# The adaLN conditioning product of a two-layer decoder trunk: from VectorE multiply-adds to TensorE column strips

## The chip, the cores and the metric

The kernel runs on one core of a Trainium2 chip. The metric is the device time in microseconds of one execution, from the first to the last instruction of the program. The core has five engines with queues of their own: TensorE (PE in the profile; PEld is its weight load), VectorE (DVE), ScalarE (ACT), GpSimd (POOL) and SyncE (SP), which here issues most DMAs.

## The reference, in short

Two residual layers over 512 positions of 1024 channels. Each layer takes six vectors of 1024 numbers (shift, scale and gate of its two sub-layers) from a conditioning vector `c`:

```
cond = silu(c)                                   # (1, 1024)
for layer in range(2):
    mod = cond @ w_ada[layer] + b_ada[layer]     # w_ada[layer]: 1024 x 6144
    sh1, sc1, g1, sh2, sc2, g2 = split(mod, 6)
    u = rms_norm(h, norm_mix[layer]) * (1 + sc1) + sh1
    mix = attention and convolution of u @ w_in, times w_out   # layer 0
        or the multi-scale pooling mixer                       # layer 1
    h = h + g1 * mix
    u = rms_norm(h, norm_ffn[layer]) * (1 + sc2) + sh2
    h = h + g2 * grouped_moe(u)                  # 16 experts, top 2
out = rms_norm(h, norm_final)
```

Everything is fp32. The product with `w_ada` is a vector times a matrix: 50.3 MB are read, and each number is used once.

## The kernel before

Every engine has one instruction stream, and its order is written out by hand; semaphores tie the streams together. The order around the change is this.

*First stage.* SyncE loads `x` (four tiles of 512 KB) and the first six chunks of `w_ada`. A chunk is 384 columns of all 1024 rows, 1.5 MB, loaded as two halves of four rows per partition (`load_ada`); there are two chunk buffers, `adaw`. The rows 8p to 8p + 7 of the matrix lie on partition p, so the 128 partitions read places 192 KB apart, in both kernels. ScalarE and VectorE normalise the four tiles of `x` (`norm`). Then VectorE multiplies and adds (`ada_mul`, lines 812 to 838): for each k, 128 x 384 weights times the partition's `cond[:, k]`, into two accumulators, which it adds at the end. In the first six chunks two of the eight k go to TensorE instead (line 1203, one output row). TensorE then sums the accumulator over the partitions with a column of ones (`ada_total`, line 1206, one output row of `ps5`), ScalarE copies the row and stores it to `mod_dram` (`ada_out`). When six chunks, 2304 columns, are stored, GpSimd reads shift and scale back by columns (`load_cols`), VectorE makes the scale, ScalarE and VectorE spread the normalised and transposed tiles (`spread_all`), and the projections begin (`project`, line 1314).

*Projections and attention.* Six projections of 128 output channels come first, then nine rounds (units) of attention: scores, the transposed probabilities of the unit before, a projection, the attention product, a projection. Units 6 to 8 have no projections; halves of the output product (`mix_half`, line 1373) stand in their place. Between these pieces are 33 places, six after the projections and three per unit, and the lists `BY_PROJ` and `BY_UNIT` say how many of the remaining 26 chunks VectorE takes in at each:

```
BY_PROJ = [1, 1, 1, 1, 2, 2]
BY_UNIT = [1, 1, 0, 1, 1, 1, 1, 1, 0, 1, 1, 1, 1, 1, 0, 1, 1, 1, 1, 1, 0, 1, 0, 0, 0, 0, 0]
```

TensorE's totals and ScalarE's copies follow up to two chunks later at the same places (`place_totals`). SyncE's queue holds, in order, the chunks and between them the five pieces of `w_in` (9.4 MB) and the two of `w_out` (3 MB and 1 MB); it waits where a buffer isn't free yet, and everything behind it waits too. A place's VectorE work on attention is `soften` (lines 912 to 930: the added distance penalty, the maxima and small operations) and `divide`; its share of the projections is `empty`.

*After.* From about 306 us on come the routing, the 16 experts of layer 0 from 341 us, and layer 1. None of this is touched, but the pooling matrices and the scale of layer 1 are loaded into the space of `adaw` once the last chunk has been used.

Of the kernel before, what the change touches and what calls it, by code (L numbers as in the profile page):

```python
# [26 lines left out]
ALU = mybir.AluOpType  # L27
# [14 lines left out]
MACS = [sum(K_VEC[:n]) for n in range(LAYERS * NCH + 1)]  # L42
# [25 lines left out]
def trunk(nc, x, c, w_ada, b_ada, norm_mix, norm_ffn, w_in, w_out, sinks, conv_w, w_pool, pool_scale,  # L68
          w_router, b_router, w_gate, w_up, w_down, norm_final, consts, pool_mats, out, mod_dram, xhat_dram, h_dram):
    ctx = ExitStack()  # L70
    with ctx:
# [32 lines left out]

        adaw = sb("adaw", [P, 2, KD, AC])
        wpool = adaw[:, 0].rearrange("p k n -> p (k n)")[:, 0:KD * 256].rearrange("p (a n) -> p a n", a=KD)
        pmat = adaw[:, 1].rearrange("p k n -> p (k n)")[:, D:D + 4 * M_END].rearrange("p (g n) -> p g n", g=4)
        acc = sb("acc", [P, 4, AC])
        brow = sb("brow", [P, 2, AC])
        mrow = sb("mrow", [1, 2, AC])  # L110
# [48 lines left out]
        psc = adaw[:, 1].rearrange("p k n -> p (k n)")[:, 0:D]  # L159
        gmix = [gbc[:, :], acc[:, :, :].rearrange("p a n -> p (a n)")[:, 0:D]]  # L160
# [8 lines left out]
        craw = sb("craw", [P, KD])  # L169
        modc = sb("modc", [P, 4, 2, KD])  # L170
# [37 lines left out]
        ada_in = [sem(f"ada_in{b}{half}") for b in range(2) for half in "ab"]  # L208
# [6 lines left out]
        mac_step = sem("mac_step")  # L215
        ada_mac = sem("ada_mac")
        ada_sum = sem("ada_sum")
        row_copied = sem("row_copied")
# [74 lines left out]
        assert N_FIRST + sum(PLACES) == LAYERS * NCH  # L293

        def place_chunks(i):
            at = N_FIRST + sum(PLACES[:i])
            return range(at, at + PLACES[i])

        def place_totals(i):
            def summed(i):  # L300

                if i < 0:
                    return N_FIRST
                if i == len(PLACES) - 1:
                    return LAYERS * NCH
                return max(N_FIRST, place_chunks(i - 2).stop if i >= 2 else 0, place_chunks(i).stop - LAG)
            return range(summed(i - 1), summed(i))
# [4 lines left out]
        WO_AT = [18, 28]  # L312

        def mod_waits(eng, n):

            for q in (n, n - 1):
                eng.wait_ge(mod_stored[q % 2], 16 * (q // 2 + 1))
# [43 lines left out]
        def _(sp):  # L361
            def load_ada(n):

                b, l, q = n % 2, n // NCH, n % NCH
                if n == 0:
                    sp.wait_ge(brow_clear, 1)
                for half in range(2):
                    ks = slice(half * KD // 2, (half + 1) * KD // 2)
                    if n >= 2:

                        sp.wait_ge(mac_step, MACS[n - 1] if half else MACS[n - 2] + KD // 2)
                        if half and K_VEC[n - 2] < KD:
                            sp.wait_ge(ada_sum, n - 1)
                    sp.dma_start(adaw[:, b, ks], w_ada[l, :, q * AC:(q + 1) * AC].rearrange("(p k) n -> p k n", k=KD)
                                 [:, ks]).then_inc(ada_in[2 * b + half], 16)
                    if half == 0:
                        sp.dma_start(brow[0:1, b, :], b_ada[l:l + 1, q * AC:(q + 1) * AC]).then_inc(ada_in[2 * b], 16)
# [22 lines left out]

            for n in range(N_FIRST):
                load_ada(n)

            wsrc = w_in[0].rearrange("(p k) n -> p k n", k=KD)
            sp.dma_start(win_qkv[:, :, 0:2 * P], wsrc[:, :, 0:2 * P]).then_inc(win_in["q"], 16)
# [4 lines left out]
            for n in range(N_FIRST, LAYERS * NCH):  # L410
# [16 lines left out]
            sp.wait_ge(ada_mac, LAYERS * NCH)  # L427
# [40 lines left out]
        def _(pool):  # L468
            def load_cols(s, last_chunk):

                l, half = s // 2, s % 2
                mod_waits(pool, l * NCH + last_chunk)
# [7 lines left out]
            def load_gate(l, half):  # L480
                off = (3 * half + 2) * D
                mod_waits(pool, l * NCH + ((off + D - 1) // AC))
# [3 lines left out]
            load_cols(0, N_FIRST - 1)  # L486
# [8 lines left out]
            for l in range(LAYERS):  # L495
                if l == 0:
                    load_cols(1, (5 * D - 1) // AC)
# [6 lines left out]
                if l == 0:  # L504

                    load_cols(2, N_FIRST - 1)
                    load_cols(3, (5 * D - 1) // AC)
                    mod_waits(pool, LAYERS * NCH - 1)
                    load_gate(1, 0)
# [55 lines left out]
        def _(act):  # L565
# [26 lines left out]
            def ada_out(n):  # L592

                b, l, q = n % 2, n // NCH, n % NCH
                act.wait_ge(ada_sum, n + 1)
                if n >= 2:
                    act.wait_ge(mod_stored[b], 16 * (n // 2))
# [1023 lines left out]
```

## Time and profile before

| | us |
|---|---|
| median of 3 runs | 823.69 |
| lowest and highest run | 820.74, 826.4 |
| span of the profiled execution, first to last instruction | 823.5 |
| TensorE busy in it | 699.7 |
| VectorE busy in it | 384.1 |
| ScalarE, GpSimd busy | 181.9, 115.1 |
| first projection starts at | 59.4 |
| routing starts near, experts of layer 0 near | 306, 341 |

The profiled execution is known by its span, and that span lies among the three runs. Busy time of an engine is the union of its instructions. The granted clock is the share of TensorE's full clock, 2.4 GHz, in a stretch: 1.00 is that level and 0.50 the lower one of 1.2 GHz. An fp32 matmul of 512 columns leaves two records, one per pass. The last number of a window row is what the DMA engines moved, in GB/s. "A <- B" behind a waiting instruction names who released it.

### The profile page before, as it was taken

What the parts mean: (1) busy time and instruction counts of PE and PEld (TensorE: products, weight loads), DVE (VectorE), ACT (ScalarE), POOL (GpSimd) and SP (SyncE); (2) the same over time, 40 slices, a digit from 0 to 9 for tenths busy, and PEclk for the clock granted to TensorE, in tenths of its full rate; (3) what the DMA queues carried; (4) which work ended last, traced back from release to release, by engine and by line L of the source; (5) the groups of instructions that cost most, each with busy time, mean ns of one, the idle gap of its engine ahead of it and who ended that gap; (6) DMA issues with size and microseconds to landing.
All of it is one profiled execution on the core that took longest, in us unless ns stands there. A gap on an engine that the chain in (4) does not pass through costs nothing. (4 is left out here: it accounts for less than half of the span.)

```text
span 823.5 us, 7489 instructions
## 1 busy us (share of the span) xinstructions
PE 699.7 (85%) x2448; PEld 359.3 (44%) x2448; DVE 384.1 (47%) x796; ACT 181.9 (22%) x468; POOL 115.1 (14%) x90
## 2 busy tenths in 40 slices
PE   1569969999999994799999999479559999999960
PEld 0224434444444454455455554168534555445530
DVE  1756479998996245522232222225563323233222
ACT  3021113222221222221122211155221221122212
POOL 0000000010111003212212221100220122221110
PEclk9989969999999995799999999889559999999995
DMA  8759999865866129648888992297531889888526
GB/s 279 234 197 371 374 356 319 294 192 167 270 210 254 75 103 354 240 172 322 307 317 318 335 338 69 34 371 300 217 117 62 319 331 334 318 315 311 172 33 218
DMA packets 74977, 204.27 MB, mean 248 GB/s; under 512 B 13185, under 2 KB 48193, under 8 KB 62657
## 3 DMA queue, kind: packets, MB, share of 16 engines
q1 hardware_dynamic: 59872, 183.60, 59.7%
q0 software_dynamic: 10160, 19.46, 9.6%
q10 hardware_dynamic: 4912, 0.82, 0.6%
q8 instruction: 16, 0.26, 0.1%
q14 instruction: 17, 0.13, 0.0%
HBM read 193.04 MB, written 27.31 MB: 268 GB/s over the span
## 5 line engine op out<-in xcount | busy, mean ns | idle before, releaser
L1461 PE MATMUL ps<-ring,work 128*128 128x512 f32 x384 | 169.1, 593 | 0.0
L1314 PE MATMUL psY<-xu,ring 128*128 128x512 f32 x272 | 122.7, 606 | 1.5 <-ACT xu L627 1.5
L1461 PEld LDWEIGHTS ps<-ring,work 128*128 128x128 f32 x384 | 73.0, 191 | 90.0 <-issue 89.9
L834 DVE SCALAR_TENSOR_TENSOR acc<-adaw,cond,acc 128x384 f32<-128x384 f32 x180 | 98.6, 611 | 4.5 <-DMA adaw<-in_w_ada_dram 4.4
L1090 DVE TENSOR_TENSOR work<-work,ps 128x256 f32<-128x256 f32 x32 | 13.5, 421 | 177.9 <-ACT work L731 177.8
L522 POOL DMA_INDIRECT h_dram<-work x32 | 50.6, 1581 | 304.0 <-DVE work L1109 275.7
L1484 PE MATMUL psY<-ring,work 128*128 128x512 f32 x192 | 86.6, 594 | 1.2 <-ACT work L741 1.2
L1314 PEld LDWEIGHTS psY<-xu,ring 128*128 128x128 f32 x272 | 51.2, 193 | 69.1 <-issue 66.2
L1109 DVE SCALAR_TENSOR_TENSOR work<-psY,work,gbc 128x512 f32<-128x512 f32 x64 | 45.1, 746 | 74.0 <-PE psY L1484 74.0
L731 ACT ACTIVATE work<-ps 128x256 f32<-128x256 f32 x32 | 12.3, 385 | 270.6 <-PE ps L1461 270.6
L725 ACT ACTIVATE work<-psA,modc,scl 128x128 f32<-128x128 f32 x120 | 45.2, 457 | 51.5 <-PE psA L1451 51.5
L1461 PE MATMUL ps<-xu,work 128*128 128x512 f32 x128 | 56.2, 592 | 0.0
L1484 PEld LDWEIGHTS psY<-ring,work 128*128 128x128 f32 x192 | 34.6, 190 | 36.0 <-issue 34.4
L1083 DVE TENSOR_SCALAR work<-psA,scl,modc 128x128 f32<-128x128 f32 x120 | 41.0, 404 | 15.7 <-PE psA L1451 14.6
L1206 PE MATMUL ps<-acc,cst 128*1 128x384 f32 x64 | 29.1, 539 | 18.5 <-DVE acc L838 15.5
L1373 PE MATMUL psY<-ring,work 128*128 128x512 f32 x96 | 42.8, 597 | 1.8 <-DVE h L872 1.8
L533 POOL DMA_INDIRECT work<-xhat_dram,work x32 | 35.5, 1110 | 46.6 <-DVE work L1070 37.5
L1461 PEld LDWEIGHTS ps<-xu,work 128*128 128x128 f32 x128 | 24.3, 190 | 30.6 <-issue 30.6
L1451 PE MATMUL psA<-cst,work 128*128 128x128 f32 x240 | 33.4, 284 | 3.1 <-DMA work<-xhat_dram,work 3.1
L493 POOL TENSOR_TENSOR work<-work,sm 128x1024 f32<-128x1024 f32 (+1 forms) x8 | 14.3, 1790 | 155.2 <-DVE sm L936 155.2
L598 ACT ACTIVATE mrow<-ps 1x384 f32<-1x384 f32 x32 | 15.2, 476 | 92.5 <-PE ps L1206 90.1
L828 DVE SCALAR_TENSOR_TENSOR acc<-adaw,cond,brow 128x384 f32<-128x384 f32 x32 | 21.4, 668 | 25.7 <-DMA brow<-in_b_ada_dram 25.5
(154 smaller groups left out, 696.1 us busy)
## 6 DMA issues: line engine op xcount, KB each, us to landing
adaw<-in_w_ada_dram SPq DMA_DIRECT2D x64, 768.0 KB, 6.1
ring<-in_w_gate_dram SPq DMA_DIRECT2D x24, 1024.0 KB, 4.9
ring<-in_w_up_dram SPq DMA_DIRECT2D x24, 1024.0 KB, 7.0
ring<-in_w_down_dram SPq DMA_DIRECT2D x24, 1024.0 KB, 11.4
ring<-in_w_in_dram SPq DMA_DIRECT2D x4, 2048.0 KB, 13.6
xu<-in_w_gate_dram SPq DMA_DIRECT2D x8, 1024.0 KB, 4.8
xu<-in_w_up_dram SPq DMA_DIRECT2D x8, 1024.0 KB, 6.9
xu<-in_w_down_dram SPq DMA_DIRECT2D x8, 1024.0 KB, 11.3
```

Source lines behind the costliest of these rows:

```text
L522: pool.indirect_dma_start(out=h_dram[l], out_offset=bass.IndirectOffsetOnAxis(tok_i[:, e:e + 1], 0), in_=yrow[:, e % 2, :], in_offset=None ...
L533: pool.indirect_dma_start(out=xg[:, e % 4, :], out_offset=None, in_=xhat_dram[l], in_offset=bass.IndirectOffsetOnAxis(tok_i[:, e:e + 1], 0 ...
L725: ins = act.activation(xgT[:, j % 2, k, :], turned_ps(e)[:, k * P:(k + 1) * P], ACT.Identity, scale=scl[:, 2 * l + 1, k:k + 1], bias=modc[ ...
L834: ins = dve.scalar_tensor_tensor(part, adaw[:, b, k, :], cond[:, k:k + 1], part, ALU.mult, ALU.add)
L1083: ins = dve.tensor_scalar(xgT[:, j % 2, k, :], turned_ps(e)[:, k * P:(k + 1) * P], scl[:, 2 * l + 1, k:k + 1], modc[:, 2 * l + 1, 0, k:k + 1],
L1109: ins = dve.scalar_tensor_tensor(yrow[:, j % 2, a * 512:(a + 1) * 512], psY[:, a * 512:(a + 1) * 512], gslot[:, bass.ds(e, 1)], gbc[:, a * ...
L1206: pe.matmul(ps5[0:1, 0:AC], ones[:, 0:1], acc[:, n % 3, :], start=(K_VEC[n] == KD), stop=True).then_inc(ada_sum, 1)
L1314: ins = pe.matmul(bank, wt, uT[:, k, :], start=(k == 0), stop=(k == KD - 1))
L1373: ins = pe.matmul(ps[:, a * 512:(a + 1) * 512], lhs, wo[:, q, a * 512:(a + 1) * 512], start=(q == 0), stop=(q == 7))
L1451: ins = pe.transpose(turned_ps(e)[:, k * P:(k + 1) * P], xg[:, j % 4, :].rearrange("p (a k) -> p k a", k=KD)[:, k, :], ident)
L1461: ins = pe.matmul(gu_ps[j % 2][:, :].rearrange("p (a f) -> p a f", a=2), xgT[:, j % 2, k, :], w_gu(j % 4)[:, :, k, :], start=(k == 0), sto ...
L1484: ins = pe.matmul(psY[:, a * 512:(a + 1) * 512], hT[:, q, :], w_dn(j)[:, q, a * 512:(a + 1) * 512], start=(q == 0), stop=(q == 1))
```

## The change

The conditioning product goes to TensorE altogether. `cond` is widened once to 32 equal columns (`condw`). The matrix is taken in slices of 1 MB: one of the eight rows of each partition, 2048 columns wide, one run of 8 KB per partition. Eight slices make a bank of 2048 columns, there are three banks per layer, 48 slices in all, and three buffers of a slice. For each slice TensorE runs four matmuls, each of 512 columns and with 32 equal stationary columns, into the four strips of 32 partitions of `ps5`; over the eight slices they accumulate, so that partitions 0, 32, 64 and 96 hold the row. VectorE adds the bias from PSUM (`row_sum`), and ScalarE stores the four pieces (`row_out`). The order of SyncE's loads, the places and the transposes of the first stage move with it, and SyncE no longer waits for the first shift and scale ahead of the second piece of `w_in`. Shortened where "..." stands:

```diff
-AC = 384
-NCH = MODW // AC
-N_FIRST = 6
-K_VEC = [KD - 2 if n < N_FIRST else KD for n in range(LAYERS * NCH)]
+AC = 512
+AG = 4
+BANK = AG * AC
+NB = MODW // BANK
+NSL = LAYERS * NB * KD
+ABUF = 3
...
+        condw = sb("condw", [P, KD, 32])
...
-        LAG = 2
-        BY_PROJ = [1, 1, 1, 1, 2, 2]
-        BY_UNIT = [1, 1, 0, 1, 1, 1, 1, 1, 0, 1, 1, 1, 1, 1, 0, 1, 1, 1, 1, 1, 0, 1, 0, 0, 0, 0, 0]
+        BY_PROJ = [1, 1, 2, 2, 2, 2]
+        BY_UNIT = [2, 2, 1] * 6 + [0] * 9
...
-        WO_AT = [18, 28]
+        WO_AT = [21, 46]
...
             def load_ada(n):
...
+                b, bank, k = n % ABUF, n // KD, n % KD
+                l, q = bank // NB, bank % NB
+                if n >= ABUF:
+                    sp.wait_ge(ada_mm, n - ABUF + 1)
+                sp.dma_start(adaw[:, b, :], w_ada[l, :, q * BANK:(q + 1) * BANK].rearrange("(p k) n -> p k n", k=KD)
+                             [:, k]).then_inc(ada_in[b], 16)
+                if k == 3:
+                    if bank == 0:
+                        sp.wait_ge(brow_clear, 1)
+                    else:
+                        sp.wait_ge(row_ready, bank)
+                    sp.dma_start(brow[0:P:32, :],
+                                 b_ada[l, q * BANK:(q + 1) * BANK].rearrange("(a n) -> a n", a=AG)
+                                 ).then_inc(brow_in, 16)
...
-            for n in range(N_FIRST):
+            wsrc = w_in[0].rearrange("(p k) n -> p k n", k=KD)
+            for n in range(KD):
+                if n == KD - 2:
+                    sp.dma_start(win_qkv[:, :, 0:2 * P], wsrc[:, :, 0:2 * P]).then_inc(win_in["q"], 16)
                 load_ada(n)
...
-            sp.wait_ge(modc_in[0], 32)
             sp.dma_start(win_qkv[:, :, 2 * P:B0], wsrc[:, :, 2 * P:B0]).then_inc(win_in["qkv"], 16)
...
-                for name, place, dst, at0 in (("c", 3, win_c, C0), ("x", 4, win_x, X0), ("b", 5, win_b, B0)):
-                    if n == N_FIRST + place:
+                for name, place, dst, at0 in (("c", 4, win_c, C0), ("x", 6, win_x, X0), ("b", 8, win_b, B0)):
+                    if n == KD + place:
...
+            def row_out(n):
+
+                l, q = n // NB, n % NB
+                act.wait_ge(row_ready, n + 1)
+                act.dma_start(mod_dram[l, q * BANK:(q + 1) * BANK].rearrange("(a n) -> a n", a=AG),
+                              mrow[0:P:32, n % 2, :]
+                              ).then_inc(mod_stored[n % 2], 16)
...
+            def row_sum(n):
...
+                dve.wait_ge(ada_mm, (n + 1) * KD)
+                dve.wait_ge(brow_in, 16 * (n + 1))
+                if n >= 2:
+                    dve.wait_ge(mod_stored[b], 16 * (n // 2))
+                dve.tensor_tensor(mrow[:, b, :], ps5[:, :], brow[:, :], ALU.add).then_inc(row_ready, 1)
...
+            def ada_slice(n):
+
+                bank, k = n // KD, n % KD
+                if n == 0:
+                    pe.wait_ge(condw_ready, 1)
+                if k == 0 and bank:
+                    pe.wait_ge(row_ready, bank)
+                pe.wait_ge(ada_in[n % ABUF], 16 * (n // ABUF + 1))
+                for a in range(AG):
+                    ins = pe.matmul(ps5[32 * a:32 * a + 32, :], condw[:, k, :],
+                                    adaw[:, n % ABUF, a * AC:(a + 1) * AC], start=(k == 0), stop=(k == KD - 1))
+                ins.then_inc(ada_mm, 1)
...
-            for n in range(N_FIRST):
-                if n == 2:
+            for n in range(KD):
+                if n == 4:
                     transposes_all(range(KD - 1))
-                ada_total(n)
-            pe.wait_ge(row_copied, N_FIRST)
+                ada_slice(n)
+            pe.wait_ge(row_ready, 1)
             keep_clock(4, ps5[:, :])
             transposes_all(range(KD - 1, KD))
```

At the places TensorE calls `ada_slice` for each slice of `place_slices`, and VectorE and ScalarE call `row_sum` and `row_out` where the eighth slice of a bank stands.

## Rows read from the trace of the kernel before

**Rows 1.** Windows: span, busy PE, PEld, DVE, ACT, POOL; clock, DMA share, GB/s.
```profile
0.00:59.43 59.43, 26.76 (x77) 8.09 (x77) 29.90 (x60) 13.98 (x26) 1.53 (x6) 0.94 0.72 230
59.43:114.00 54.57, 47.41 (x156) 22.68 (x156) 29.76 (x58) 5.99 (x11) 0.53 (x1) 0.96 1.05 374
114.00:127.80 13.80, 11.78 (x28) 4.85 (x28) 13.59 (x31) 3.88 (x12) 0.00 (x0) 0.68 0.92 301
127.80:231.20 103.40, 102.17 (x339) 45.22 (x338) 94.64 (x190) 24.15 (x72) 10.23 (x6) 1.00 0.73 243
231.20:306.00 74.80, 72.95 (x255) 35.28 (x254) 41.49 (x82) 21.37 (x54) 5.13 (x4) 1.00 0.47 170
```
**Rows 2.** TensorE's waits (total, times, longest), 56 to 125 us, then 118 to 300.
```profile
PE ps L1206 <- DVE acc L838: 7.4, 2, 5.4
...
PE ps L1206 <- DVE acc L838: 2.0, 1, 2.0
...
PE ps L1206 <- ACT mrow L598: 1.2, 1, 1.2
```
**Rows 3.** Timeline to the first projections: start, duration, engine, line.
```profile
21.14 0.75 DVE L843 TENSOR_SCALAR xu<-h,rstd 128x1024 f32<-128x1024 f32 x1
...
50.30 1.21 PE L1206 MATMUL ps<-acc,cst 128*1 128x384 f32 x2
52.08 3.70 PE L1193 MATMUL ps<-cst 128*128 128x512 f32 x8 [0.57 <-ACT mrow L598]
53.46 1.33 POOL L478 DMA_DIRECT2D modc<-mod_dram  x2 [52.93 <-DMA mod_dram<-mrow]
59.43 20.84 PE L1314 MATMUL psY<-xu,ring 128*128 128x512 f32 x48 [1.53 <-ACT xu L627]
```
**Rows 4.** Timeline of TensorE, the end of the first projections.
```profile
112.64 1.44 PE L1206 MATMUL ps<-acc,cst 128*1 128x384 f32 x2 [5.42 <-DVE acc L838]
...
117.27 1.44 PE L1206 MATMUL ps<-acc,cst 128*1 128x384 f32 x2 [2.02 <-DVE acc L838]
118.64 9.17 PE L1314 MATMUL psY<-xu,ring 128*128 128x512 f32 x16
```
**Rows 5.** Timeline of TensorE, the end of unit 3 and the start of unit 4.
```profile
182.19 1.58 PE L1354 MATMUL ps<-work 128*64 128x128 f32 x16
183.70 7.13 PE L1314 MATMUL psY<-xu,ring 128*128 128x512 f32 x16
190.77 0.81 PE L1206 MATMUL ps<-acc,cst 128*1 128x384 f32 x2
191.50 1.14 PE L1329 MATMUL psA<-work 64*128 64x256 f32 x8
...
192.57 0.66 PE L1341 MATMUL ps<-cst,work 128*128 128x128 f32 x4
```
**Rows 6.** Groups by line, 59 to 272 or 310 us: busy, mean ns, idle before.
```profile
L1206 PE MATMUL ps<-acc,cst 128*1 128x384 f32 x52 | 22.2, 510 | 10.4 <-DVE acc L838 7.4 <-ACT mrow L598 3.0
...
L834 DVE SCALAR_TENSOR_TENSOR acc<-adaw,cond,acc 128x384 f32<-128x384 f32 x156 | 85.0, 610 | 0.1
...
L910 DVE TENSOR_TENSOR work<-work,psY 128x512 f32<-128x512 f32 x4 | 2.7, 670 | 0.6 <-PE psY L1314 0.6
L921 DVE SCALAR_TENSOR_TENSOR work<-cst,psA 128x128 f32<-128x128 f32 x8 | 1.8, 281 | 0.0
...
L926 DVE TENSOR_REDUCE sm<-work 128x4 f32<-128x512 f32 x2 | 1.4, 686 | 0.1
```
**Rows 7.** Windows as in rows 1: x, chunks alone, expert weights.
```profile
2.00:10.00 8.00, 0.00 (x0) 0.00 (x0) 0.51 (x3) 1.33 (x2) 0.00 (x0) 1.00 0.99 365
10.00:18.00 8.00, 2.72 (x4) 0.37 (x4) 0.92 (x2) 3.97 (x8) 0.00 (x0) 1.00 1.07 330
...
320.00:324.00 4.00, 0.22 (x8) 0.23 (x9) 3.60 (x13) 0.00 (x0) 0.00 (x0) 0.50 1.01 427
```
**Rows 8.** Window inside line 1354's block: PE and PEld busy, clock, DMA share, GB/s.
```profile
182.70:183.00 0.30, 0.30 (x8) 0.30 (x8) 1.00 0.45 159
```

More of the change, by code:

```diff
@@ L103, in w_dn @@
             return wslot(j)[:, 2 * KD * FF:SLOT].rearrange("p (a d) -> p a d", a=2)
[L105 to L110, printed above, removed]
+        adaw = sb("adaw", [P, ABUF, BANK])
+        wpool = adaw[:, 0].rearrange("p (a n) -> p a n", a=KD)
+        pmat = adaw[:, 1, 0:4 * M_END].rearrange("p (g n) -> p g n", g=4)
+        gm1 = sb("gm1", [P, D])
+        brow = sb("brow", [P, AC])
+        mrow = sb("mrow", [P, 2, AC])
         gbc = sb("gbc", [P, D])
@@ L207, in trunk @@
         eps_ready, brow_clear = sem("eps_ready"), sem("brow_clear")
-        ada_in = [sem(f"ada_in{b}{half}") for b in range(2) for half in "ab"]
+        ada_in = [sem(f"ada_in{b}") for b in range(ABUF)]
+        brow_in = sem("brow_in")
         win_in = {part: sem(f"win_in_{part}") for part in ("q", "qkv", "c", "x", "b")}
@@ L286, in trunk, with place_slices, place_banks @@
         BESIDE = [([6], [7]), ([8], [9]), ([10], [11]), ([12], [13]), ([14], [15]), ([16], [17])] + [([], [])] * 3
-        LAG = 2
-        BY_PROJ = [1, 1, 1, 1, 2, 2]
-        BY_UNIT = [1, 1, 0, 1, 1, 1, 1, 1, 0, 1, 1, 1, 1, 1, 0, 1, 1, 1, 1, 1, 0, 1, 0, 0, 0, 0, 0]
+        BY_PROJ = [1, 1, 2, 2, 2, 2]
+        BY_UNIT = [2, 2, 1] * 6 + [0] * 9
         PLACES = BY_PROJ + BY_UNIT
-        assert N_FIRST + sum(PLACES) == LAYERS * NCH
-        def place_chunks(i):
-            at = N_FIRST + sum(PLACES[:i])
+        assert KD + sum(PLACES) == NSL
+        def place_slices(i):
+            at = KD + sum(PLACES[:i])
             return range(at, at + PLACES[i])
[L299 to L307, printed above, removed]
+        def place_banks(i):
+            return [n // KD for n in place_slices(i) if n % KD == KD - 1]
         def unit_places(u, q, what):
@@ L362, in load_ada @@
             def load_ada(n):
[L364 to L377, printed above, removed]
+                b, bank, k = n % ABUF, n // KD, n % KD
[12 more added lines that the diff above has]
+                                 ).then_inc(brow_in, 16)
             def load_expert(l, e, j):
@@ L468, in _, with load_cols @@
         def _(pool):
-            def load_cols(s, last_chunk):
+            def load_cols(s):
                 l, half = s // 2, s % 2
-                mod_waits(pool, l * NCH + last_chunk)
+                mod_waits(pool, l * NB + ((3 * half + 2) * D - 1) // BANK)
                 off = 3 * half * D
@@ L649, in _ @@
                 norm(0, t)
[L650 to L651 removed]
+            row_out(0)
             spread_all()
@@ L699, in _ @@
                 empty(m)
-                for n in place_totals(m):
-                    ada_out(n)
+                for n in place_banks(m):
+                    row_out(n)
             for u in range(ATT_U + 1):
@@ L877, in _ @@
             dve.memset(eps[:, :], EPS).then_inc(eps_ready, 1)
-            dve.memset(brow[:, :, :], 0.0).then_inc(brow_clear, 1)
+            dve.memset(brow[:, :], 0.0).then_inc(brow_clear, 1)
             dve.wait_ge(cond_ready, 1)
+            dve.tensor_copy(condw[:, :, :], cond[:, :].unsqueeze(2).broadcast_to([P, KD, 32])).then_inc(condw_ready, 1)
             dve.wait_ge(const_in, 16)
@@ L884, in _ @@
                 norm(0, t)
-            for n in range(N_FIRST):
-                ada_mul(n)
+            row_sum(0)
             dve.wait_ge(small_in, 16 * N_SMALL)
@@ L938, in _ @@
             for m in range(6):
-                for n in place_chunks(m):
-                    ada_mul(n)
+                for n in place_banks(m):
+                    row_sum(n)
             for u in range(ATT_U):
@@ L1193, in keep_clock @@
                     pe.matmul(bank, ident, cst[:, 0:512], start=True, stop=True)
-            def ada_total(n):
-                if n:
-                    pe.wait_ge(row_copied, n)
-                if K_VEC[n] < KD:
-                    pe.wait_ge(ada_in[2 * (n % 2) + 1], 16 * (n // 2 + 1))
-                    pe.wait_ge(cond_ready, 1)
-                    for k in range(K_VEC[n], KD):
-                        pe.matmul(ps5[0:1, 0:AC], cond[:, k:k + 1], adaw[:, n % 2, k, :], start=(k == K_VEC[n]),
-                                  stop=False)
-                pe.wait_ge(ada_mac, n + 1)
-                pe.matmul(ps5[0:1, 0:AC], ones[:, 0:1], acc[:, n % 3, :], start=(K_VEC[n] == KD), stop=True
-                          ).then_inc(ada_sum, 1)
+            def ada_slice(n):
[9 more added lines that the diff above has]
+                ins.then_inc(ada_mm, 1)
             def transposes_all(ks):
@@ L1379, in _ @@
                 project(m)
-                for n in place_totals(m):
-                    ada_total(n)
+                for n in place_slices(m):
+                    ada_slice(n)
             for u in range(ATT_U + 1):
```

104 lines of the change are left out of this document (33 added, 71 removed).

## The prediction

> **What bounds the kernel now.** I read the stages first, then what TensorE waited for, then its instructions one by one around the change, and the DMA rates last. Only the first 306 us hold work that the change touches. In the stage table [rows 1] see three different limits. To 59.4 us TensorE is busy 26.8 us and nothing flows evenly: the modulation row is being made. From 59.4 to 114 the DMA engines are full (374 GB/s, share 1.05), with TensorE close behind. From 127.8 to 306 TensorE is busy 102.2 of 103.4 and 73.0 of 74.8 us; DMA has room (243 GB/s). VectorE is busy 94.6 of 103.4 us there too, but the waits [rows 2] say that this costs TensorE almost nothing after 118 us: 2.0 us for VectorE and 1.2 for ScalarE's row copy. Over both windows it is 7.4 us for VectorE, the 2.0 among them, and 3.0 for ScalarE [rows 6]. So VectorE's multiply-adds in this stretch (85.0 us in the L834 group alone, [rows 6]) are nearly all covered by TensorE: releasing VectorE buys the waits and no more, while each microsecond put on TensorE is paid in full.
>
> **The first row.** Its last total starts at 50.30 and lasts 1.21; then come ScalarE's copy, the store, POOL's gather at 53.46, the spreading, and the first projection at 59.43 [rows 3]: 7.9 us from the last total. After the change a DVE addition (0.67 us for 512 columns, the L910 row of [rows 6]) takes the place of a 0.48 us copy: 8.1 us. What comes ahead is now a stream: x 2.10 MB, the constants 0.41, eight slices of 1.05 and the first piece of w_in 1.05, 11.95 MB in all, against 13 MB in the same place before. The queue starts near 2 us, moves 365 GB/s to 10 us and 330 with the old chunks alone [rows 7]; at 345 that is 36.6 us, 1.2 more for landing and 1.2 for the last product: 39.0. The first projection then starts at 47.1, **12.3 us earlier**. TensorE is no obstacle: at half clock a slice takes about 1.9 us against 3.0 us of DMA, but the 28 transposes stand ahead of slice 4 and can't start before the last norm, begun at 21.14 [rows 3], ends, so it can't come before about 36. Bounds: 15 us earlier if slices move at the 427 GB/s of the expert weights [rows 7], which also have 8 KB per partition; 7 us earlier at 300 GB/s, or if the four clock-keeping matmuls, which took 3.70 us [rows 3], run at half clock and hold up the last transposes.
>
> **What TensorE gets.** Forty slices remain after the first row. A 512-column fp32 matmul is two passes: 48 records in 20.84 us [rows 3] is 0.43 us a pass, 0.86 us a matmul. Four of them, one per strip of 32 columns, make a slice. Do the strips run together? Nothing in the trace uses four. The nearest rows are the attention products, whose outputs are two strips of 64: sixteen passes of 128 columns fill 1.51 us, from 182.19 to the next block at 183.70 [rows 5]. One after the other they need 16 x 0.11, with 0.2 for the changes of shape 1.95 us. In the middle 0.30 us eight of these records are under way [rows 8], about twice what a single stream could show. The scores, two strips of 64 rows, take 1.07 us for eight passes of 256 columns [rows 5], and 1.9 would be serial. So strips overlap, two at full rate; I take the same for four: 0.86 us a slice, 34.3 us for forty, and 0.1 to enter each of the 24 places, 2.4. The second strips of the attention block begin late; at the worst that is 0.37 us a place, 8.9 in all, at best nothing; I take 2.4. **Added: 39.1 us.** Without any overlap a slice costs 3.43 us, with pairs 1.72: these are the upper bounds. Below 0.86 nothing goes, since one strip's own two passes take it.
>
> The Trainium skill speaks of this ("TensorE: Matmul & The Clock Gate", section "Measured speedup vs the span model"): three strips of 32 columns reached 2.38x, not 3x. By that ratio a slice would be an estimated 1.08 us and the sum 9 us higher; no run here shows it. The trace's two strips lose less.
>
> **What it loses.** Twenty-six totals in this stretch (x52, [rows 6]) take 0.73 us each from start to start (190.77 to 191.50, [rows 5]): 19.1 us, and 0.5 for changes of shape that vanish in the last units. The twelve products of the first stage are in the first term. The waits ahead of these totals are 10.4 us [rows 6]. The wait of 5.4 us before 112.64 also brought half clock: the projection at 118.64 took 9.17 us instead of 7.13, the totals on its two sides 1.44 instead of 0.81 [rows 4, 5], with the scores between them 3.4 us; clock over that stretch 0.68 [rows 1]. **Removed: 19.6 + 10.4 + 3.4 = 33.4 us.**
>
> **What it waits for next.** Three buffers of 1 MB let the queue run at most three slices ahead, and a slice's load is issued only when the one three before it is consumed. The stretch up to the first attention unit is the tight one: from 2 us until slice 19, 33 MB must pass, 88 us at 374 GB/s [rows 1], and by this plan TensorE asks for slice 19 near 98 us; but during the first projections, with single slices, the queue runs dry for some 10 us in all. So about 2 us are lost at slice 19. Then the 3.1 MB of w_out are queued ahead of slice 21: slice 20, w_out and 21 are 5.2 MB, 14 us, while TensorE has a projection and two slices, 8 to 9 us: 5 us lost. Together 7 (0 with the queue at 427, 15 at 330). From here to the end a unit moves 5 slices in about 20 us, 262 GB/s, and keeps up. The 1 MB second part of w_out before slice 46 fits too. A wait of 5 us is what made the clock fall before [rows 2, 4]; if it does again, 2.5 us (0 to 5). Last, slices 23 and 24 share a place and belong to two banks of columns: TensorE must wait for VectorE's sum of bank 2, which stands behind the softmax preparation of that unit (four additions at 281 ns, a reduction of 686 and small ones, [rows 6], some 3 us) while TensorE has 1.6 us to do: 2.5 us (0 to 4). Behind it wait that unit's projections and ScalarE's store; no other bank boundary falls inside one place but 7 us apart. **New waits: 12 us.**
>
> The brow loads (four rows of 2 KB, 6 instead of 32) and the six row stores lie beside other work; if not, each delays one bank and not the path. The narrower clearing of brow and the widening of cond to 32 columns are over before slice 0 lands. POOL's loads for the later norms find their rows stored earlier than now; they have slack. The second stage's sources (pool scale, gate) only change place.
>
> **Sum.** -12.3 + 39.1 - 33.4 + 12 = +5.4 us. The profiled span is 823.5 us, 0.2 under the median of the three runs and inside their spread of 5.7, so I add it there: **829 us**. A measurement of this kernel can tell about 1%, 8 us, from no change.
>
> **Rivals.**
> 1. *Strips together, small waits* (the sum): 829, own range 821 to 838. Chance 0.45, of which 0.33 within 1% and 0.12 slower.
> 2. *The queue keeps up.* If 8 KB pieces move as the expert weights do (427 GB/s), the start gains 15, the DMA wait and the clock loss vanish: -15 + 39.1 - 33.4 + 2.5, and with no late strips -2.4: -9.2, so 814. For it: same piece size. Against: the old chunks have the same distance of 192 KB between partitions and moved at 330 [rows 7]. Chance 0.25: 0.18 faster, 0.07 within.
> 3. *Starved by three buffers*: the waits spread from unit 0 to the first slices, 15 us and clock 5, start only 8 earlier, the bank wait as before: -8 + 39.1 - 33.4 + 22.5 = +20, so 844. It decides when slices move below 330 GB/s. The Trainium skill has a rule on this side ("DMA: Bandwidth & Descriptors", section "Latency and other measured facts"): rows 512 KiB apart moved at 207 GB/s. Slices here lie 192 KB apart, as the chunks do, and those moved faster. Chance 0.15, slower.
> 4. *TensorE becomes dearer*: the strips run in pairs or one at a time. Forty slices cost 34 us more (about 860) or 103 more (about 925, since then no DMA wait is left). It decides as soon as a slice takes over 1.1 us. For it: in the attention block the second strips begin only when half of the first are through; four were never tried. Against: the scores' strips begin together. Chance 0.15, slower.
>
> **Numbers.** Faster 0.18 (case 2, with 0.02 from a start better than taken): 0.2; within 1% 0.33 + 0.07: 0.4; slower 0.12 + 0.15 + 0.15: 0.4. The range takes in cases 1 to 3 and their bounds, and leaves out most of case 4 and the tip of 2: 812 to 855.
>
> **What would show it.** The first projection near 47 us, else the first term is wrong. The product's block for a place of two slices: 1.9 us right, 3.6 pairs, 7 serial. TensorE waits on adaw after project 5 and at slice 21, on VectorE's sum at slice 24, and a half-clock stretch after slice 21, or none of them. VectorE's busy time before 306 us down by more than the 85 us of L834 [rows 1, 6], with no other wait of TensorE for it. From 306 us on (less the shift) everything as before; a difference there would break the argument.

## The result, and the profile after

The changed kernel takes 845.23 us (median of 4 runs, 844.0 to 850.49), the kernel before 825.05 in the same series: ratio 1.026 with the interval 1.022 to 1.030, so slower. The time lies in the predicted range (812 to 855) and beyond my likeliest case (829). The profiled execution took 844.98 us, its span is 843.3; before it was 823.5, so 19.8 us are to be explained where I had summed 5.4.

The page's first part, and the group of the product, for the changed kernel:

```profile
PE 719.2 (85%) x2744; PEld 367.1 (44%) x2744; DVE 240.0 (28%) x527; ACT 167.1 (20%) x436; POOL 114.2 (14%) x90
...
L1176 PE MATMUL ps<-adaw,condw 128*32 128x512 f32 x384 | 52.6, 647 | 32.8 <-DMA adaw<-in_w_ada_dram 30.2
```

VectorE's busy time fell from 384.1 us to 240.0, and the kernel is slower all the same. The stages of the changed kernel, cut at the same pieces of work as [rows 1] (columns as there):

```profile
0.00:57.19 57.19, 24.43 (x104) 10.19 (x105) 8.77 (x20) 11.10 (x20) 1.53 (x6) 0.79 0.82 303
57.19:118.39 61.20, 56.87 (x248) 25.44 (x249) 3.09 (x11) 6.61 (x16) 1.18 (x2) 0.97 0.76 285
118.39:132.06 13.67, 10.82 (x36) 3.86 (x33) 0.00 (x0) 0.60 (x1) 0.39 (x1) 0.88 1.02 415
132.06:251.00 118.94, 116.43 (x510) 48.85 (x507) 31.01 (x72) 17.86 (x58) 8.61 (x5) 0.97 0.61 228
251.00:325.68 74.68, 72.19 (x256) 36.00 (x255) 22.41 (x47) 18.69 (x48) 4.83 (x4) 1.00 0.29 114
```

The first stage is 2.2 us shorter, not 12.3. The second is 6.6 us longer and the fourth and fifth together 15.4: there TensorE has the slices. The routing begins at 325.68 instead of 305.94, and from there on both kernels need 517.6 us. So all of the loss is before it: -2.2 to the first projection and +22.0 from there to the routing.

TensorE's waits (total, times, longest) of the changed kernel from 57.5 to 326 us, to be held against [rows 2]:

```profile
PE ps L1176 <- DMA adaw<-in_w_ada_dram: 7.2, 4, 2.8
PE ps L1176 <- DVE mrow L810: 2.5, 1, 2.5
PE psY L1344 <- DVE h L844: 2.5, 2, 1.9
```

The predicted DMA waits (7) and the wait at the boundary of two banks (2.5) are there. TensorE's timeline shows what they did to the clock:

```profile
57.19 8.95 PE L1285 MATMUL psY<-xu,ring 128*128 128x512 f32 x16 [1.12 <-ACT xu L619]
66.07 1.06 PE L1176 MATMUL ps<-adaw,condw 128*32 128x512 f32 x8
67.06 7.13 PE L1285 MATMUL psY<-xu,ring 128*128 128x512 f32 x16
...
82.19 1.92 PE L1176 MATMUL ps<-adaw,condw 128*32 128x512 f32 x16
84.04 7.13 PE L1285 MATMUL psY<-xu,ring 128*128 128x512 f32 x16
...
117.39 1.06 PE L1176 MATMUL ps<-adaw,condw 128*32 128x512 f32 x8 [2.34 <-DMA adaw<-in_w_ada_dram]
118.39 8.83 PE L1285 MATMUL psY<-xu,ring 128*128 128x512 f32 x16
...
131.06 1.06 PE L1176 MATMUL ps<-adaw,condw 128*32 128x512 f32 x8 [2.85 <-DMA adaw<-in_w_ada_dram]
132.06 8.83 PE L1285 MATMUL psY<-xu,ring 128*128 128x512 f32 x16
...
146.64 1.94 PE L1176 MATMUL ps<-adaw,condw 128*32 128x512 f32 x8 [2.51 <-DVE mrow L810]
148.50 7.69 PE L1285 MATMUL psY<-xu,ring 128*128 128x512 f32 x16
```

Two readings. A place with one slice takes 0.99 us from start to start (66.07 to 67.06), one with two 1.85 (82.19 to 84.04): the four strips run together. And behind each of four stretches with waits (the late first row, then those ahead of 117.39, 131.06 and 146.64) comes a piece at half clock (1.2 instead of 2.4 GHz): projections of 8.95, 8.83 and 8.83 us instead of 7.13, then a slice of 1.94 instead of 1.06 and half a microsecond behind it, 6.6 us in all.

Where the first stage's gain went is seen in its chain. All engines of the changed kernel, from the last slice to the first projection:

```profile
40.20 1.77 PE L1176 MATMUL ps<-adaw,condw 128*32 128x512 f32 x8 [2.03 <-DMA adaw<-in_w_ada_dram]
...
42.01 0.69 DVE L810 TENSOR_TENSOR mrow<-ps,brow 128x512 f32<-128x512 f32 x1 [13.80 <-PE ps L1176]
42.74 1.06 ACTq L590 DMA_DIRECT2D mod_dram<-mrow  x1
...
48.06 1.33 POOL L473 DMA_DIRECT2D modc<-mod_dram  x2 [47.54 <-DMA mod_dram<-mrow]
53.92 0.17 DVE L820 SCALAR_TENSOR_TENSOR scl<-modc,normc 128x8 f32<-128x8 f32 x1 [11.22 <-DMA modc<-mod_dram]
```

The last slice ends at 41.97 (I had 39.0). The store of 8 KB then takes 5.3 us from issue to POOL's gather, the gather 5.9 us to VectorE's scale. Before, the last store (1.5 KB) took 1.4 us to the gather at 53.46 [rows 3], and the gather 2.7 us to the scale:

```profile
52.05 0.22 ACTq L600 DMA_DIRECT2D mod_dram<-mrow  x1
...
56.16 0.17 DVE L848 SCALAR_TENSOR_TENSOR scl<-modc,normc 128x8 f32<-128x8 f32 x1 [6.70 <-DMA modc<-mod_dram]
```

The windows from 42 to 50 us of the changed kernel, then of 50 to 58 in the kernel before, tell why:

```profile
42.00:50.00 8.00, 5.92 (x8) 2.25 (x8) 0.69 (x1) 0.00 (x0) 1.33 (x2) 0.67 1.04 414
```

```profile
50.00:58.00 8.00, 5.92 (x15) 2.09 (x13) 1.81 (x4) 2.12 (x4) 1.33 (x2) 0.93 0.10 10
```

SyncE had waited for the first shift and scale before it issued the second piece of `w_in`. That wait had kept the DMA engines free (10 GB/s) for two tiny transfers on which everything stood. Without it they share with 414 GB/s of matrix. By this reading, theory A below, the removed wait costs 6 to 7 us. A second loss is in the first stage's slices, where ScalarE's queue is in play:

```profile
10.87 2.18 ACTq L577 DMA_DIRECT2D brb<-in_b_router_dram  x1
13.08 6.08 ACTq L583 DMA_DIRECT2D snk<-in_sinks_dram  x4
...
21.66 1.04 ACT L609 ACTIVATE work<-h 128x1024 bf16<-128x1024 f32 x1
...
34.06 1.92 PE L1176 MATMUL ps<-adaw,condw 128*32 128x512 f32 x16
```

ScalarE stands at the issues of its eleven small loads until 20.2 us; the first norm starts at 21.66, before at 15.36. The transposes follow the norms and hold TensorE until 34.06, and behind them slices 4 and 5 run without a wait for their loads: they were there. Only then was slice 7's load issued (at 35.18, with slice 4 consumed), and it is the one used at 40.20. Beside this, the loads themselves stood still for a while. From 16 to 18 us SyncE's queue (q1) moves almost nothing while the small pieces of ScalarE's (q10) go (queue: packets, MB, share of time):

```profile
q10 hardware_dynamic: 1510, 0.08, 50.9%
q1 hardware_dynamic: 29, 0.11, 13.2%
```

### The profile page after: what moved, and what is told of

It is laid out like the page before. It is cut to its first block and busy times, and to the rows that moved or that the text cites. A ratio compares the mean times of both kernels' runs of the same rounds, so it can differ in the third digit from the quotient of the medians.

```text
span 843.3 us, 7594 instructions
## 1 busy us (share of the span) xinstructions
PE 719.2 (85%) x2744; PEld 367.1 (44%) x2744; DVE 240.0 (28%) x527; ACT 167.1 (20%) x436; POOL 114.2 (14%) x90
## 5 line engine op out<-in xcount | busy, mean ns | idle before, releaser
L1285 PE MATMUL psY<-xu,ring 128*128 128x512 f32 x272 | 127.0, 622 | 1.1 <-ACT xu L619 1.1
L1176 PE MATMUL ps<-adaw,condw 128*32 128x512 f32 x384 | 52.6, 647 | 32.8 <-DMA adaw<-in_w_ada_dram 30.2
L722 ACT ACTIVATE work<-ps 128x256 f32<-128x256 f32 x32 | 12.3, 384 | 271.1 <-PE ps L1432 271.1
L1062 DVE TENSOR_TENSOR work<-work,ps 128x256 f32<-128x256 f32 x32 | 13.5, 421 | 177.8 <-ACT work L722 177.8
L1176 PEld LDWEIGHTS ps<-adaw,condw 128*32 128x32 f32 x384 | 9.1, 111 | 61.5 <-issue 30.8
L1422 PEld LDWEIGHTS psA<-cst,work 128*128 128x128 f32 x240 | 30.3, 193 | 6.1 <-DMA work<-xhat_dram,work 6.1
L1455 PE MATMUL psY<-xu,work 128*128 128x512 f32 x64 | 28.9, 595 | 2.6 <-ACT work L732 2.6
```

Of the source, the lines that this page charges most:

```text
L1062: dve.tensor_tensor(hid[:, j % 2, :], sil[:, j % 2, :], gu_ps[j % 2][:, FF:2 * FF], ALU.mult).then_inc(hid_ready, 1)
L1176: ins = pe.matmul(ps5[32 * a:32 * a + 32, :], condw[:, k, :], adaw[:, n % ABUF, a * AC:(a + 1) * AC], start=(k == 0), stop=(k == KD - 1))
L1285: ins = pe.matmul(bank, wt, uT[:, k, :], start=(k == 0), stop=(k == KD - 1))
L1422: ins = pe.transpose(turned_ps(e)[:, k * P:(k + 1) * P], xg[:, j % 4, :].rearrange("p (a k) -> p k a", k=KD)[:, k, :], ident)
L1455: ins = pe.matmul(psY[:, a * 512:(a + 1) * 512], hT[:, q, :], w_dn(j)[:, q, a * 512:(a + 1) * 512], start=(q == 0), stop=(q == 1))
```

## The experiments

Medians, with the ratio to the kernel before measured on the same chip and its 95% interval; the last column is the start of the first projection in the profiled execution.

| kernel | median us | ratio | first projection |
|---|---|---|---|
| before | 825.05 | 1 | 59.43 |
| after | 845.23 | 1.026 [1.022, 1.030] | 57.19 |
| e1_wait_back | 840.72 | 1.017 [1.012, 1.023] | 51.16 |
| e2_norms_first | 845.06 | 1.024 [1.020, 1.028] | 57.35 |
| e3_2kb_pieces | 851.69 | 1.032 [1.027, 1.036] | 60.69 |
| e4_before_no_wait | 822.65 | 0.998 [0.996, 1.000] | 62.40 |
| e5_small_loads_late | 831.74 | 1.009 [1.007, 1.011] | 43.33 |
| e6_late_and_spread | 826.42 | 1.003 [1.001, 1.005] | 43.16 |
| e7_before_small_late | 826.23 | 1.001 [0.999, 1.004] | 47.35 |
| e8_one_strip | 943.96 | 1.145 [1.138, 1.152] | 66.91 |
| e9_best_of_change | 815.08 | 0.986 [0.983, 0.990] | 40.46 |
| e10_before_both | 823.18 | 0.997 [0.995, 1.000] | 53.36 |
| e11_places_alone | 832.28 | 1.012 [1.007, 1.017] | 57.43 |

### SyncE's wait

**e1_wait_back**, the changed kernel with one line ahead of the second piece of `w_in`:

```diff
+            sp.wait_ge(modc_in[0], 32)
```

> The changed kernel with SyncE's old wait for shift and scale back ahead of the second piece of w_in, so that this piece and slices 8 to 10 are issued only when GpSimd's gather has landed. Theory A (the store and the gather of the first row are late because the DMA engines are full of SyncE's loads just then, 414 GB/s from 42 to 50 us against 10 GB/s in the kernel before): store 1.4 us instead of 5.3, gather 2.6 instead of 5.8, first projection near 50 instead of 57.2, and, since the queue stood idle from 58 to 67 us anyway, nearly all of it is kept: 838 us. Rival B (the prefetch is worth as much as the early row): the first projection comes at 50, but the waits for slices 16 to 21 grow by the same 7 us: 845.

Its gather and its scale:

```profile
45.26 1.33 POOL L474 DMA_DIRECT2D modc<-mod_dram  x2 [44.73 <-DMA mod_dram<-mrow]
```

```profile
47.89 0.17 DVE L821 SCALAR_TENSOR_TENSOR scl<-modc,normc 128x8 f32<-128x8 f32 x1 [4.72 <-DMA modc<-mod_dram]
```

The store, issued at 43.20, takes 2.1 us and the gather 2.6, with 3 GB/s moved from 42 to 48 us. The first projection comes 6.0 us earlier and 5.0 of them still stand at the last block before routing (317.2 for 322.2). The removed wait's price is shown; it is a quarter of the loss.

**e4_before_no_wait**, the kernel before without that wait:

```diff
-            sp.wait_ge(modc_in[0], 32)
```

> The kernel before without SyncE's wait for shift and scale ahead of the second piece of w_in; its chunks and w_in move in pieces of 1 to 2 KB. Theory A (turns by piece): store and gather share the engines with small pieces and lose 1 to 3 us in all, and the early prefetch gives some of it back from the 9 us of TensorE waits before 118 us: 822 to 826. Rival B (only the amount queued counts): store and gather lose the same 7 us as in the changed kernel: first projection near 66, 828 to 832.

The gather begins at 53.10 and its data is used at 59.13: 6.0 us instead of 2.7, and the projection at 62.40 is 3.0 later, so that part repeats. Yet the last block before routing starts at 296.5 instead of 302.5. TensorE's waits from 62.5 to 306 us say where from:

```profile
PE ps L1205 <- ACT mrow L597: 3.5, 3, 1.7
PE psY L1372 <- DVE h L871: 1.9, 1, 1.9
```

The 7.4 us for VectorE [rows 2] are gone, and the half clock after them: with the loads a few microseconds ahead, its chunks are done in time. What had made VectorE late were loads. In the kernel before it waits for them in the same stretch (59.3 to 272 us; all but 0.1 us of it before 108), ahead of the first instruction of a chunk:

```profile
L828 DVE SCALAR_TENSOR_TENSOR acc<-adaw,cond,brow 128x384 f32<-128x384 f32 x26 | 17.7, 680 | 24.6 <-DMA brow<-in_b_ada_dram 24.5
```

The bias row named there and the first half of its chunk count on one semaphore, and both stand in SyncE's queue, with the DMA engines full (share 1.05 [rows 1]). In e4 VectorE waits 0.4 us for loads from 62.5 to 118 us. The same edit costs at the start and gives back later, in the kernel that has the later wait to give back (span 817.9, the fastest run of ten; over the runs it is no more than 2 us).

### The small loads and the norms

**e2_norms_first**, ScalarE's four norm blocks issued ahead of its eleven small loads (`act` block, order only):

```diff
-            for s in range(4):
-                ... the 11 small loads
             ... the norms
+            for s in range(4):
+                ... the 11 small loads
```

> The changed kernel with ScalarE's four norms ahead of its eleven small loads, not behind them. Theory A (ScalarE stands at its issues until 20 us, because its small pieces take turns with 8 KB pieces; the norms, the 28 transposes and slice 4 wait for it): norms begin near 9 us instead of 21.7, transposes before 20, slice 4 follows slice 3 at once, last slice of the first row 4 to 5 us earlier, 841 us. Rival B (the slices' loads are what the first row waits for): norms early, last slice within 1 us of now, 845; or the small loads become late themselves and the scale waits for them, 848.

The norms begin at 5.26 us, 16 us earlier, and nothing comes of it. TensorE in this kernel:

```profile
30.45 1.82 PE L1176 MATMUL ps<-adaw,condw 128*32 128x512 f32 x8 [2.98 <-DMA adaw<-in_w_ada_dram]
37.64 1.94 PE L1176 MATMUL ps<-adaw,condw 128*32 128x512 f32 x8 [5.37 <-DMA adaw<-in_w_ada_dram]
40.33 1.94 PE L1176 MATMUL ps<-adaw,condw 128*32 128x512 f32 x8 [0.75 <-DMA adaw<-in_w_ada_dram]
```

The hole in the stream of slices has moved from slice 3 to slices 5 and 6, together with the small loads; the last slice ends at 42.3. So early norms alone buy nothing, and late norms alone are not what binds: the small loads take the queue wherever they stand.

**e3_2kb_pieces**, the same slices loaded as 2 KB runs, four per partition and slice (a padded buffer):

```diff
-        adaw = sb("adaw", [P, ABUF, BANK])
+        adaw = sb("adaw", [P, ABUF, AG * (AC + 16)])
```

> The changed kernel with 16 unused columns behind each 512 in the slice buffer, so that a slice is written in pieces of 2 KB instead of 8 KB. Nothing else changes. Theory A (a DMA engine takes one piece from each queue in turn, so small pieces move at the pace of the large ones beside them): ScalarE's small loads are through by 14 us, not 20, the store and the gather of the first row take some 5 us instead of 11, first projection near 48 to 50, 837 us; the 1 MB loads themselves no slower than 5 per cent. Rival B (it is only how much is queued): issues, store and gather as now, 845, or slower if 2 KB pieces move more slowly.

With small packets on both queues ScalarE is through at 14.9 us instead of 20.2, so the size of SyncE's pieces does hold up ScalarE's issues. The rest is worse: slice 3 comes at 30.23 instead of 24.82, and store and gather stay slow. In this kernel:

```profile
30.23 1.93 PE L1180 MATMUL ps<-adaw,condw 128*32 128x512 f32 x8 [9.81 <-DMA adaw<-in_w_ada_dram]
```

```profile
51.74 1.33 POOL L477 DMA_DIRECT2D modc<-mod_dram  x2 [51.22 <-DMA mod_dram<-mrow]
```

The store issued at 46.64 takes 5.1 us, the gather 5.7. What slows them is how much is queued, not the size of its pieces: one rival less.

**e5_small_loads_late**, e1 with ten of the small loads after the first row's store and the spreading, and the first norm weights on the early semaphore (VectorE's wait for the other ten moves behind the spreading too):

```diff
-        N_SMALL = 11
+        N_SMALL = 10
...
+            sp.wait_ge(modc_in[0], 32)
...
+            act.dma_start(normc[:, 0, :], norm_mix[0].rearrange("(p k) -> p k", k=KD)).then_inc(c_in, 16)
...
+            ... the other 10 small loads, after row_out(0) and spread_all()
```

> e1 (SyncE's wait back) with ten of ScalarE's eleven small loads behind the first row and its spreading; only the norm weights that the first scale needs stay ahead, in one contiguous load, and VectorE waits for the rest after the spreading. Theory C (while ScalarE's queue works through thousands of 4-byte pieces, SyncE's loads hardly move: 0.11 MB from 16 to 18 us with two slices issued): slices 3 to 7 land at 3 us each, norms begin near 6 us, the last slice of the first row is through at 35 to 37 us instead of 42, first projection near 45 instead of 51.2, 835 us. Rival D (the three buffers and the clock set the pace of the first row): last slice at 40 or later, 839 to 841.

Now the slices run at full rate where they had stood still (16 to 18 us: 94 GB/s in the changed kernel), in this kernel:

```profile
16.00:18.00 2.00, 1.45 (x12) 0.20 (x8) 0.00 (x0) 0.00 (x0) 0.00 (x0) 1.00 1.00 418
```

The last slice ends at 34.5 and the first projection starts at 43.33: 7.8 us before e1's. This and e1's 6.0 together start it earlier than the 47.1 that I had predicted. The edit frees the queue and lets the norms begin early at once; e2 shows that the norms alone give nothing, the free queue with late norms was not tried.

**e7_before_small_late**, the same move in the kernel before (its SyncE wait stays). **e10_before_both**, that and no SyncE wait.

> The kernel before with the same move of the ten small loads. Theory C: its queue had nothing to load from 18 to 24 us, because VectorE was busy with norms; with the norms done by 12 us VectorE begins its multiply-adds 9 us sooner, the first projection comes 6 to 9 us sooner, 817 us. Rival: VectorE is through its norms but the chunks are what it waits for, 1 to 3 us, 822.

> The kernel before with both of the small moves: no wait of SyncE ahead of the second piece of w_in, and ten of ScalarE's small loads behind the spreading. e4 alone was 0.2 per cent faster, e7 alone the same, since VectorE's multiply-adds then held up the totals near 100 us. If the two add up (the early queue feeds what the early norms allow) 818; if VectorE is the limit up to 120 us whatever the start, 823. It tells whether TensorE strips are worth anything against the old split with the same care in the first stage.

In e7 the first projection starts 12.1 us earlier (47.35) and the total does not move. Its TensorE waits from 46 to 300 us:

```profile
PE ps L1208 <- DVE acc L839: 18.6, 4, 8.2
```

They were 7.4 for VectorE. But it is not VectorE's pace that takes the head start. Its own timeline in e7:

```profile
68.69 0.17 DVE L892 TENSOR_SCALAR snk<-snk 128x8 f32<-128x8 f32 x1 [21.44 <-DMA cvw<-in_conv_w_dram]
```

The edit put VectorE's wait for the ten late loads behind the spreading and so ahead of all its multiply-adds. It stands there for 21.4 us, no chunk buffer comes free, and the loads run dry (40 GB/s from 65 to 70 us, 374 in the kernel before). A further 16.4 us up to 118 are waits for chunks and bias rows. In e10 it stands 11.6 us at the same line. So e7 and e10 do not show what a quicker start is worth in the kernel before: the edit itself took the head start away. The same edit with that wait just ahead of the attention was not tried. e10 gives 2.4 us before routing and 0.3% over the runs. In the changed kernel VectorE has nothing to do at that time, so its 40.3 us at the same line (e5) hold nobody up, and the quicker start is kept: 5.0 of e1's 6.0 us, 5.1 of e5's 7.8.

### The strips and the places

**e8_one_strip**, the changed kernel with all four matmuls into the first strip, three of them with zero columns as stationary: three quarters of each row are left out. The four clock-keeping matmuls of the first stage write the first strip only, too.

```diff
-                    ins = pe.matmul(ps5[32 * a:32 * a + 32, :], condw[:, k, :], ...
+                    ins = pe.matmul(ps5[0:32, :], condw[:, k, :] if a == 0 else condz[:, :], ...
```

> The changed kernel with all four matmuls of a slice in strip 0. Strips 1 to 3 are left out of the row: their three matmuls have a stationary operand of zeros, so those columns of the modulation hold the bias alone; the clock-keeping matmuls write strip 0 too. Theory F (the strips run side by side, and that is why a slice costs 0.86 us): a place of two slices takes 7 us instead of 1.86, TensorE has 103 us more, and no wait for a slice is left, so 843 + 103 - 15 = about 930. Rival (the four passes would overlap within one strip as well, or were never side by side): near 845.

```profile
75.64 1.04 PE L1179 MATMUL ps<-adaw,condw 128*32 128x512 f32 x2
76.53 2.74 PE L1179 MATMUL ps<-adaw,condz 128*32 128x512 f32 x6
79.19 6.28 PE L1289 MATMUL psY<-xu,ring 128*128 128x512 f32 x14
```

One after the other, a slice takes 3.55 us (75.64 to 79.19) for 0.99, and the kernel 99 us more. Rival 4 is refuted: the strips of the change do run together.

**e6_late_and_spread**: e5 with the slices and the two parts of w_out spread more evenly.

```diff
-        BY_PROJ = [1, 1, 2, 2, 2, 2]
-        BY_UNIT = [2, 2, 1] * 6 + [0] * 9
+        BY_PROJ = [1, 1, 1, 1, 2, 2]
+        BY_UNIT = [2, 1, 1] * 8 + [0] * 3
-        WO_AT = [21, 46]
+        WO_AT = [28, 38]
```

> e5 with the 40 slices spread over the places so that none is asked for sooner than the queue can have it: 8 in the projections, then 2, 1 and 1 in each of units 0 to 7, no bank boundary inside a place, and the two pieces of w_out behind slices 28 and 38. Theory E (after the first projection the change loses 9 us in waits on slices, 2.5 at the bank boundary and some 4 in the half clock that follows): these go, the products cost the same 38 us, and the time is 12 to 16 us under e5: 820 to 823. Rival (the waits are only moved, into units 6 and 7 or to w_out): 830 to 835.

**e11_places_alone**: the changed kernel with e9's places, nothing else. **e9_best_of_change**: those places on top of e5, and the first piece of `w_in` behind the eighth slice instead of the sixth.

```diff
+        BY_PROJ = [1, 1, 1, 1, 1, 1]
+        BY_UNIT = [1, 1, 1] + [2, 1, 1] * 4 + [2, 2, 1] * 3 + [0] * 3
+        WO_AT = [26, 36]
```

> The changed kernel with only e9's places and w_out loads; the first stage stays as the change has it (no wait of SyncE, small loads ahead of the norms, first piece of w_in ahead of slice 6). If the two losses are independent, the first projection stays at 57 and the stretch from it to the end of the output product shortens from 265 to about 250 us, as in e9: 828 to 830. If the places help only once the first stage is early (more time for the queue to run out), the gain is more than that: 825; if they help only then by hiding its waits, less: 836.

> e6 taken further: the first piece of w_in behind slice 7 instead of ahead of slice 6, and the slices thinned where e6 still waited for one issued only at the place before: one in each of the six projections and in each place of unit 0, then 2, 1, 1 in units 1 to 4 and 2, 2, 1 in units 5 to 7. Theory E: the last slice of the first row comes 3 us sooner (first projection near 40 instead of 43.2), the 5 us of waits near 100 us and the half clock after them go, 818 us, the first version with the change that beats the kernel before. Rival (the projections then begin before w_in's pieces are there, or units 5 to 7 wait): 824.

e6 still waits 5.7 us on slices. In e11 no slice is waited for once the projections have begun, and the clock stays at full level from 60.9 us to the routing; and from a first projection at 57.4 the last block before routing starts at 307.5 instead of 322.2. In e9, from 41 to 293 us, TensorE has these waits:

```profile
PE psY L1346 <- DVE h L845: 1.9, 1, 1.9
PE psY L1287 <- ACT xu L607: 1.5, 1, 1.5
PE ps L1178 <- DMA adaw<-in_w_ada_dram: 0.7, 1, 0.7
```

and this window from 40 to 290 us, TensorE busy 247.0 of 250 us at a granted clock of 1.00:

```profile
40.00:290.00 250.00, 246.98 (x1034) 110.41 (x1035) 55.90 (x129) 43.15 (x123) 15.04 (x11) 1.00 0.69 255
```

The parts add up: e5 has 13.5 us of the changed kernel's median, e11 13.0, the order of the `w_in` piece about 3 (first projection at 40.46 for 43.33), and e9 has 30.1 of it. It beats the kernel before by 1.4% [1.0 to 1.7], e4 by 7.6 us between their medians, on different chips, and e10 by 8.1 us on the same chip. Neither e4 nor e10 is the best that the kernel before can do with the same care, since e10 has VectorE's wait in it.

## Why the prediction was right or wrong

**The first row (-12.3; measured -2.2, outside its own bounds of 7 to 15): this is the step that failed.** "What comes ahead is now a stream", priced as bytes over a rate with a chain of 8.1 us behind it. The last slice ended 3.0 us late. "TensorE is no obstacle" did not hold: ScalarE stood at its small loads, the last norm ended at 28.2 instead of 21.9, and slice 4 waited behind the transposes until 34.06. And the stream stood still at 16 to 18 us beside those loads (e5: with them moved it ends at 34.5, 4.5 before my 39.0; 404 GB/s from 10 to 32 us, not 345). And the chain took 15.2 us instead of 8.1 (e1: 8.7 us from the end of the last slice, with the wait back; its store of 8 KB takes 2.1 us, that of 1.5 KB before took 1.4). I named the removed SyncE wait in the description of the change and gave it no term: a wait that is taken away lets more into the queue, and two small transfers on which everything stood then moved beside 414 GB/s. The two together are the 10.1 us.

The row that I called the old chunks alone (330 GB/s [rows 7]) was not alone: ScalarE's queue moved 1712 packets in it. From 34 to 42 us, with 4 such packets, the chunks moved 322, so the rate was right for them. It was not the rate of pieces of 8 KB.

**Added on TensorE (39.1; measured 37.6): right.** Sixteen places of two slices at 1.85 and eight of one at 1.0. The strips' records start 6 to 7 ns apart. The ratio of 2.38 for three strips, which the Trainium skill gives ("TensorE: Matmul & The Clock Gate", "Measured speedup vs the span model") and which would have made a slice an estimated 1.08 us, isn't borne out by it: a second slice adds 0.86, and 3.44 in e8, a ratio of 4.0, the full four strips (3.6 for a place of one slice, 3.55 over 0.99). The same section's model, one matmul's duration and some 4 ns for each further strip, is near; the trace has 6 to 7 ns.

**Removed (33.4): right within the balance, not measured by itself.** The 7.4 us "for VectorE" in it were waits for loads one step further back (e4 above). From the first projection to the routing the added 37.6, less 33.4, with 7.2 and 2.5 of new waits, 6.6 of clock and 0.3 of small waits give 20.8 us; 22.0 were measured. The 1.2 stay unassigned.

**New waits (12; measured 16.3).** DMA 7.2 for 7, at the places named (behind the projections, and beside w_out). The bank boundary of slices 23 and 24: 2.51 for 2.5, at 146.64, behind the softmax preparation as said. The clock was the mis-sized term: 6.6 for 2.5. I took one fall behind a wait of 5 us. There were four pieces at half clock and no such wait between them: one behind the late chain (clock 0.67 from 42 to 50 us, then a TensorE wait of 6.3), one behind waits of 1.2, 0.8 and 2.3 us between 110 and 117.4, one behind a single wait of 2.85 and one behind 2.51.

**Covered work (0): right.** 144 us less of VectorE, no term. From the routing on nothing differs.

**The rivals.** The range held, and in part by luck: its upper end was there for rival 3 and the bounds, and what made the time (a store and a gather beside full queues, small loads beside the slices) stands in no rival. The time is near rival 3's 844, but that is no proof of it: its waits were to be 15 us and its start 8 earlier; measured are 7.2 and 2.2, and the slices move above 400 GB/s when they are alone. Rival 2 was right in its rate and its early start (15 us; e5 16.1, e9 19.0) once two things outside it were mended. The lower rate that the Trainium skill gives for rows 512 KiB apart ("DMA: Bandwidth & Descriptors", "Latency and other measured facts") isn't seen at 192 KB (e5's 404 GB/s). Slower over 1% had 0.4, the highest chance together with no change.

**Open.** Whether the kernel before, with the small loads moved and VectorE's wait for them behind its multiply-adds, would come as far as e9. And why SyncE's loads hardly move while ScalarE's 4-byte pieces go. Packets go one for one between the two queues as long as both have work; from 10 to 16 us in the changed kernel:

```profile
q1 hardware_dynamic: 334, 2.47, 99.5%
q10 hardware_dynamic: 334, 0.00, 3.3%
```

That costs the big loads little. The Trainium skill has a rule for it ("DMA: Bandwidth & Descriptors", "Queues, rings and completion order"): each DMA engine takes turns between its queues, a packet at a time. The counts above agree with it; they do not show the order. But from 16 to 18 us it is 29 to 1510, and SyncE's queue is short of packets although a slice was issued at 14.28 and used only at 24.82. What holds them back was not isolated.

## What to carry to other kernels

A wait ahead of a large load may be there to keep the DMA engines free for a small transfer on the path: before it is taken away, look at what is in flight beside the smallest transfer of the chain, and at the GB/s of that window. Small loads with 4-byte pieces belong where no stream is needed, even if another engine issues them; and when they move, the wait for them has to move with them, behind the work that doesn't need them (e7's 21.4 us). When a wait names an engine, ask what that engine waited for. Moving work from a covered engine to the bounding one costs its full time (here 37.6 us against an estimated 33.4 removed). Here it paid 1.4% only with an earlier start and with the new work spread so evenly that no wait let the clock fall; whether the old split would have paid as much is open.

## What was not expected of the hardware

- A store of 8 KB takes 2.1 us with the DMA engines free (one of 1.5 KB 1.4; 3 and 10 GB/s) and 5.3 with 414 GB/s beside it; the gather of shift and scale 2.6 to 2.7 and 5.9. With 2 KB pieces beside them it is 5.1 and 5.7.
- Seven of the eleven small loads took 0.33 to 1.04 us to issue on ScalarE's queue, the other four 2.2 to 4.3 us (3402, 2186, 2181 and 4342 ns) while SyncE's queue moved `x` and the slices.
- From 16 to 18 us SyncE's queue moved 0.11 MB beside 1510 small packets, at a busy share of 0.64: the engines were not full, and the large loads stood all the same.
